# Two feed-forwards opened one token tile at a time, a gated unit's first step in two, modulation blocks at rate 1.0 in a downward product

## The reference, cut to what matters

```python
def first_block(...):                       # everything in float32
    for l in range(2):
        mod = silu(c) @ w_ada[l] + b_ada[l]             # 6 x 1024 numbers
        h = rms_norm(x, g_pre_mix[l]) * (1 + sc_m) + sh_m
        y = token_mixer(h, ...)                          # projections, two attentions, w_out
        x = x + gt_m * rms_norm(y, g_post_mix[l])
        h = rms_norm(x, g_pre_ffn[l]) * (1 + sc_f) + sh_f
        a = causal_depthwise_conv(h @ w_up_act[l], w_conv[l], b_conv[l])   # 3 taps over tokens
        y = (gelu(a) * (h @ w_up_lin[l])) @ w_down[l]    # 1024 -> 2816 -> 1024
        x = x + gt_f * rms_norm(y, g_post_ffn[l])

def _ffn_half(s, mod, g, wg, wu, wd):       # second network, 4 x 2 of these
    h = modulate(rmsnorm(s, g), shift, scale)
    return s + 0.5 * gate * ((silu(h @ wg) * (h @ wu)) @ wd)
```

## Time and profile before

| | |
|---|---|
| median of 3 runs | 2504.09 us (2496.96 to 2507.48) |
| the profiled execution | 2505.47 us, its span 2503.7 us |
| mean granted TensorE clock | 0.99 |
| TensorE matmul (PE) | 2418.9 us busy, 97%, 13166 instructions |
| weight loads (PEld) | 2036.0 us, 81% |
| VectorE (DVE) | 1676.1 us, 67% |
| ScalarE (ACT) | 1081.1 us, 43% |
| GpSimd (POOL) | 393.2 us, 16% |
| read from memory | 419.17 MB, 168 GB/s over the span |
| chain that ended last | PE 88%, DVE 6%, ACT 2%, issue 2%, POOL 1% |

### The profile page before, as it was taken

How to read it: one execution, slowest core, us unless ns; L and a number is a source line. 1 busy time by engine, 2 the same in 40 slices (tenths; PEclk the granted TensorE clock), 3 DMA queues, 4 the chain that set the end, 5 groups by cost and what they waited for, 6 DMA issues and landing times.

```text
span 2503.7 us, 34854 instructions
## 1 busy us (share of the span) xinstructions
PE 2418.9 (97%) x13166; PEld 2036.0 (81%) x13166; DVE 1676.1 (67%) x2618; ACT 1081.1 (43%) x1849; POOL 393.2 (16%) x431
## 2 busy tenths in 40 slices
PE   6999999989999999999979999999999999999998
PEld 5778987769989888887648888889888888777997
DVE  6967886869995776777955565565565556356554
ACT  4566545666554212237744322224322225345443
POOL 0211101111211201106850110100100110001101
PEclk9999999999999999999989999999999999999999
DMA  8656885556873554442112443442453443332662
GB/s 314 238 197 210 301 297 207 192 210 229 278 252 126 197 192 166 180 168 81 64 29 86 146 180 128 168 168 90 156 184 120 158 144 126 108 91 80 194 202 93
DMA packets 123336, 422.57 MB, mean 169 GB/s; under 512 B 15904, under 2 KB 20128, under 8 KB 123168
## 3 DMA queue, kind: packets, MB, share of 16 engines
q1 hardware_dynamic: 122608, 418.55, 48.2%
q10 hardware_dynamic: 560, 1.79, 0.2%
HBM read 419.17 MB, written 1.11 MB: 168 GB/s over the span
## 4 chain that ended last, share of the span: by engine, by line
PE 88%; DVE 6%; ACT 2%; issue 2%; POOL 1%; DMA 0%; DVEq 0%; ACTq 0%; POOLq 0%
PE ps L1159 27%; PE ps L1160 27%; PE ps L1161 27%; PE ps L1342 2%; PE ps L1354 2%; DVE sl L1705 1%; DVE mjunk L1719 1%; PE ps L1259 1%; PE ps L1322 1%; POOL ap L2226 1%; PE ps L1311 1%; ACT junk L1440 1%; DMA X<-in_x 0%; ACT F L1476 0%; DVE hL L1794 0%
## 5 line engine op out<-in xcount | busy, mean ns | idle before, releaser
L1417 ACT ACTIVATE sh<-raw 128x1024 fp32r<-128x1024 f32 x534 | 552.4, 1044 | 914.1 <-PE ps L1161 913.8
L1159 PE MATMUL ps<-hH,sh 128*128 128x256 f32 (+1 forms) x2560 | 840.8, 328 | 2.0 <-DVE hL L1794 2.0
L1161 PE MATMUL ps<-hH,sl 128*128 128x256 f32 (+1 forms) x2560 | 836.0, 327 | 0.0
L1160 PE MATMUL ps<-hL,sh 128*128 128x256 f32 (+1 forms) x2560 | 836.0, 327 | 0.0
L1705 DVE TENSOR_TENSOR sl<-raw,sh 128x1024 fp32r<-128x1024 f32 x534 | 640.3, 1219 | 107.0 <-ACT sh L1417 106.6
L1159 PEld LDWEIGHTS ps<-hH,sh 128*128 128x128 f32 x2560 | 481.4, 188 | 53.3 <-issue 5.6
L1160 PEld LDWEIGHTS ps<-hL,sh 128*128 128x128 f32 x2560 | 482.2, 188 | 49.3 <-issue 1.7
L1161 PEld LDWEIGHTS ps<-hH,sl 128*128 128x128 f32 x2560 | 481.2, 188 | 48.0
L1719 DVE CUSTOM_DVE_ANT_0 mjunk<-raw,cB,V 128x1024 bf16<-128x1024 f32 x384 | 499.2, 1300 | 26.6 <-DMA C<-in_cst 8.5
L2199 POOL TENSOR_TENSOR uLl<-F,uHh 128x256 fp32r<-128x256 f32 (+1 forms) x132 | 169.8, 1287 | 1172.1 <-ACT uHh L1594 1061.3
L1160 PE MATMUL ps<-sl,uHh 128*128 128x512 f32 x792 | 312.1, 394 | 0.0
(11 more groups left out here) (164 smaller groups left out, 2036.1 us busy)
## 6 DMA issues: line engine op xcount, KB each, us to landing
raw<-in_w SPq DMA_DIRECT2D x752, 512.0 KB, 4.6
G<-gates SPq DMA_DIRECT2D x14, 512.0 KB, 6.3
raw<-in_w SPq DMA_DIRECT2D x16, 256.0 KB, 4.4
cB<-in_rpb SPq DMA_DIRECT2D x64, 64.0 KB, 2.7
raw<-in_w SPq DMA_DIRECT2D x4, 492.0 KB, 6.7
S<-in_rows SPq DMA_DIRECT2D x6, 256.0 KB, 3.4
X<-in_x ACTq DMA_DIRECT2D x1, 1024.0 KB, 12.0
X<-in_ctx SPq DMA_DIRECT2D x1, 1024.0 KB, 5.9
```

The costliest lines, as they stand in the source:

```text
L1159: self.e.matmul(out, lh, rh, start=start, stop=False)
L1160: self.e.matmul(out, lh, rl, start=False, stop=False)
L1161: return self.e.matmul(out, ll, rh, start=False, stop=stop)
L1417: self.e.activation(self.m["sh"][k % SPL][:, 0:w], self.m["raw"][r % RAW][:, 0:w], ACT.Copy).then_inc(self.sems["w_hi"], 1)
```

## The change

Four parts.

- **Opening tile by tile** (`by_tile`). The first four chunks of both up products of the first layer's `ffn1`, and of gate and up of the last `ffn2`, are computed in the form of `down`: 8 units, tile 0 first, tile 1 behind it. Four banks of 128 tokens x 512 features per product come out; each is copied to SBUF (`utok`: tile 0 on ACT, tile 1 on DVE) and turned by four transposes (`uturn`) into the layout that the gated unit reads. `finish_norms` stands behind the third unit of tile 0. `warm(14)`, `warm(5)` become `warm(7)` in `ffn1` and `warm(14)` in `ffn2`.
- **Order before the first opening.** From the last use of a unit of `w_out` on (`hold`), no new unit is split until the plan says `ready`; tile 0's split (`second_parts`) moves ahead of tile 1's `gate2`; a `lower` is let out by `lowers`.
- **The gated unit of `ffn1`** (both layers): ACT's part (`glu1_a`) stands right behind the first product, DVE's part (`glu1_t`) is a step of its own behind the second. In layer 0 the gated units of chunks 0 to 3 are done beside the products of chunks 4 and 5, two beside each. In `ffn2` they stand ahead of the product of chunk 4.
- **Modulation blocks**: `RATES["down0"]` goes from 0.6 to 1.0. With four chunks fewer in the loop, `ffn1` of layer 0 has 18 calls of `pace(2)` where it had 22. `aside` starts with 6 empty items where it had 8, in both layers.

```diff
@@ RATES
-"down0": 0.6
+"down0": 1.0
@@ norm_tile(..., held=False)
         if early:
             self.second_parts()
+        if held:
+            self.add("lowers")
+            self.add("ready", n=1)
         ys = ...
         self.add("scale", ...)
@@ gate_half(..., held=False)
         self.first_parts()
         self.rms_close(st2[t], 2)
+        self.second_parts()
+        if held and t:
+            self.add("ready", n=1)
         for j in range(2):
             ...
-        self.norm_tile(hid, t, AB, 0, st, early=True)
+        self.norm_tile(hid, t, AB, 0, st, early=True, held=held and t)
@@ mixer, last product
                     part(kp, half, taken[(kp, half)], [i], i == 1, ...)
+                    if i and not half and kp == 2 and not l:
+                        self.add("hold", on=True)
-                self.gate_half(i, half, banks[half][i], gid, AB, hid, st2)
+                self.gate_half(i, half, banks[half][i], gid, AB, hid, st2, not l)
@@ new
+    def by_tile(self, names, hid, warm):
+        take = lambda n, j: self.unit(True, [n + (k, 0, 512) for k in (2 * j, 2 * j + 1)])
+        def part(n, j, t, b, last):
+            self.add("down", unit=n, ks=[2 * j, 2 * j + 1], tiles=[(t, (t, b))], last=last, full=b if j == 3 else None,
+                     act=("h", hid), nk=KD)
+        def stage(t, b, on):
+            S = self.place("S", 2 + t)
+            self.add("utok", b=b, S=S, on=on)
+            self.left(b)
+            return S
+        def turned(t, S, to):
+            self.add("uturn", S=S, t=t, to=to)
+        self.warm(warm)
+        self.add("hold", on=False)
+        one, two = ([take(n, j) for j in range(4)] for n in names)
+        A, B = [self.bank(), self.bank()], [self.bank(), self.bank()]
+        for j in range(3):
+            part(one[j], j, 0, A[0], False)
+        self.finish_norms()
+        part(one[3], 3, 0, A[0], False)
+        for j in range(2):
+            part(two[j], j, 0, B[0], False)
+        SA0 = stage(0, A[0], "a")
+        to = [self.bank(), self.bank()]
+        for j in range(4):
+            part(one[j], j, 1, A[1], True)
+            if j == 1:
+                turned(0, SA0, to)
+        for j in range(2):
+            part(two[j], j, 1, B[1], True)
+        SA1 = stage(1, A[1], "v")
+        for j in range(2, 4):
+            part(two[j], j, 0, B[0], False)
+        turned(1, SA1, to)
+        SB0 = stage(0, B[0], "a")
+        for j in range(2, 4):
+            part(two[j], j, 1, B[1], True)
+        up = [self.bank(), self.bank()]
+        turned(0, SB0, up)
+        SB1 = stage(1, B[1], "v")
+        return to, up, lambda: turned(1, SB1, up)
@@ ffn1
-        self.warm(14)
-        self.finish_norms()
-        self.warm(5)
-        self.aside += [lambda: None] * 8
+        done = 0
+        if l:
+            ...                                  # as before
+        else:
+            done = 4
+            to, up, rest = self.by_tile((("w_up_act", l), ("w_up_lin", l)), hid, 7)
+        self.aside += [lambda: None] * 6
-        for c in range(KF):
+        for c in range(done, KF):
             ba = self.product("w_up_act", l, c * 128, slice(0, 256), ("h", hid))
+            double = done <= c < done + done // 2
+            if double:
+                if c == done:
+                    rest()
+                while late:
+                    late.pop(0)()
+                begin(2 * (c - done), to[c - done], up[c - done], 0)       # glu1_a, glu1_t
+            else:
+                g = dict(...)
+                self.add("glu1_a", **g)
             if late:
                 late.pop(0)()
             bu = self.product("w_up_lin", l, c * 128, slice(0, 256), ("h", hid))
             if late:
                 late.pop(0)()
+            if double:
+                begin(2 * (c - done) + 1, to[c - done], up[c - done], 256)
+                late.pop(0)()
+                late.pop(0)()
+                begin(c, ba, bu, 0)
+            else:
+                g["bu"] = bu
+                finish(g)                                                   # glu1_t
-            self.add("glu1_a", **g)
             self.pace(2)
@@ ffn2, two tiles
-            self.warm(14)
-            self.finish_norms()
-            self.warm(5)
+            to, up, rest = self.by_tile((gate, up weights of this half), hid, 14)
@@ ffn2, loop over chunks
+                if len(tiles) == 2 and cc < 4:
+                    if c == 0:
+                        rest()
+                    ...                          # glu2_a of chunk c from to, up; glu2_b of chunk c-1
+                    continue
@@ finish
+            if s["kind"] == "hold":  held, more = s["on"], 0; continue
+            if s["kind"] == "ready": more += s["n"]
+            if s["kind"] == "lowers": out += lower; lower = []; continue
                     if split and len(order) >= SPL and order[-SPL] not in used:
                         break
+                    if split and held and not (real and n <= s["unit"]):
+                        if not more:
+                            break
+                        more -= 1
```

More of the change, by code:

```diff
@@ L225, in xs, with norm_tile @@
         return ("x", t, h, self.x_at[(t, h)])
-    def norm_tile(self, hid, t, AB, s, st=None, wide=False, lag=0, early=False):
+    def norm_tile(self, hid, t, AB, s, st=None, wide=False, lag=0, early=False, held=False):
         if st is None:
@@ L600, in ffn1 @@
                 late.pop(0)()
[L601 to L604 removed]
+            if double:
[5 more added lines that the diff above has]
+                g["bu"] = bu
+                finish(g)
             self.pace(2)
@@ L646, in ffn2 @@
                 begun = bool(head)
+                if len(tiles) == 2 and cc < 4:
+                    ba, bu, o = to[c // 2], up[c // 2], 256 * (c % 2)
+                    if c == 0:
+                        rest()
+                    g = dict(N=N, c=c, ba=ba, bu=bu, o=o, s=self.place("S", c % 2), f=self.next("F", 3), fid=fid, u=self.u_at)
+                    if late:
+                        late.pop(0)()
+                    self.add("glu2_a", **g)
+                    if c % 2:
+                        self.left(ba, bu)
+                    late.append(lambda g=g: self.add("glu2_b", **g))
+                    continue
                 if head:
@@ L653, in ffn2 @@
                         late.pop(0)()
-                g = dict(N=N, c=c, ba=ba, bu=bu, s=self.place("S", c % 2), f=self.next("F", 3), fid=fid, u=self.u_at)
+                g = dict(N=N, c=c, ba=ba, bu=bu, o=0, s=self.place("S", c % 2), f=self.next("F", 3), fid=fid, u=self.u_at)
                 if late:
@@ L919, in finish @@
         out, n, ctx, top, used, order, lower, loads = [], 0, False, 0, set(), [], [], []
+        held, more = False, 0
         for s in self.steps:
             real = "unit" in s and s["kind"] != "place"
+            if s["kind"] == "hold":
+                held, more = s["on"], 0
+                continue
+            if s["kind"] == "ready":
+                more += s["n"]
+            if s["kind"] == "lowers":
+                out += lower
+                lower = []
+                continue
             if real:
@@ L924, in finish @@
                 lower = []
-            if "unit" in s or "upto" in s:
+            if "unit" in s or "upto" in s or s["kind"] == "ready":
+                if s["kind"] == "ready":
+                    s["upto"] = len(self.units)
                 top = max(top, s["upto"] if "upto" in s else s["unit"] + 1)
@@ L1187, in warm, with uturn @@
         self.done("mm", ("left", s["b"]))
+    def uturn(self, s):
+        t, S = s["t"], self.buf(s["S"])
+        if t == 0:
+            for b in s["to"]:
+                self.wait_ge(self.gone(b))
+        self.wait_ge(self.got("tok", s["S"]))
+        for c in range(4):
+            o = 256 * (c % 2) + 128 * t
+            x = self.e.transpose(self.buf(s["to"][c // 2])[:, o:o + 128], S[:, c * 128:(c + 1) * 128],
+                                 self.m["C"][:, C_ID:C_ID + 128])
+        x.then_inc(self.sems["tr"], 1)
+        self.done("tr", ("left", s["S"]), *([("full", b) for b in s["to"]] if t else []))
     def proj(self, s):
@@ L1996, in oscale, with utok, glu1_t @@
         self.done("v_sb", ("os", s["mid"], s["kd"], s["i"]))
-    def glu1_a(self, s):
+    def utok(self, s):
+        if s["on"] != "v":
+            return
+        self.wait_ge(self.got("full", s["b"]))
+        self.wait_ge(self.gone(s["S"]))
+        self.e.tensor_copy(self.buf(s["S"])[:, :], self.buf(s["b"])[:, :]).then_inc(self.sems["v_ps"], 1)
+        self.done("v_ps", ("left", s["b"]), ("tok", s["S"]))
+    def glu1_t(self, s):
         l, c, fid = s["l"], s["c"], s["fid"]
-        S, pa = self.buf(s["s"]), self.buf(s["ba"])
+        S, pa = self.buf(s["s"]), self.buf(s["ba"])[:, s["o"]:s["o"] + 256]
         self.wait_ge(self.got("glu_a", fid, c))
```

47 lines of the change are left out of this document (34 added, 13 removed).

## The result

The changed kernel takes 2511.05 us (median of 8 runs, 2508.98 to 2514.55), the kernel before 2503.7 in the same session (8 runs, 2496.96 to 2507.48). The ratio is 1.003, its 95% interval 1.0018 to 1.0041: slower by 7 us. I had forecast 2497, with a range of 2488 to 2507.

A forecast was written before the change was run, and what follows sets the result against it. TensorE's matmuls, 88% of the chain of waits, were taken as the bound. First opening 5.6, second 1.7, `down` -0.5, layer 1's mixer 0.7 sum to 7.5: 2505.5 to 2498.0, less 1.4, say 2497; range 2488 to 2507.

The forecast's parts named there:

- Start of tile 0, wait for tile 1, W8: First opening: tile 0 starts at 199.15, tile 1 at 209.9 after waiting 1.3, chunk 4's first product (W8) at 225.4.
- Transposes: First opening: 24 transposes on TensorE at 0.11 us each, 2.64 in all; bounds 0.107 and 0.243 each.
- The rival of slow ones: Both openings: transposes take 0.243 each, losing 6.4, for 2503.0; chance 0.05.
- Made-up gated units: Beside chunks 4 and 5 of the first opening: three gated units each cost 1.0; bounds 0 and 7.0.
- the rival of splits run dry: Beside chunks 4 to 10, TensorE waits for splits and `down` begins without cover: 2507.0; chance 0.10.
- one of the signs that the prediction had named for being wrong: First opening: TensorE gaps named after `sl` between chunks 4 and 10, or tile 0's first matmul after 202.
- the 0.6 that the sum gave the form: First opening: eight units take 21.98 in the new 512-column form against 22.62 in the old, gaining 0.6.
- Last opening: Opening of the last `ffn2`: starts at 2310.95, W8 at 2335.6 in place of 2337.65; gain 1.7, bounds 0.3 and 2.1.
- `down` of layer 0 with 17 blocks: `down` of layer 0: 17 modulation blocks for 10 need 4% too much memory bandwidth; cost 0.5, bounds 0 and 2.2.
- Mixer of layer 1: Its last three blocks near 537.30 go, shortening TensorE's 1.94 wait for DVE's `hL`; gain 0.7, bounds -1.4 and 4.1.
- `glu1_a` in layer 1: Layer 1's `ffn1`: ACT's part ahead of gelu, with `aside` two items shorter, gains nothing; bounds -0.4 to 0.4.

The follow-up runs named there:

- e10: e9 with the first opening as before (both tiles together, nothing held, `down` of layer 0 at rate 0.6): 0.9994 of the kernel before.
- e9: e8 run again unchanged, for more runs and a second profile: 0.9941 of the kernel before.
- e5: Changed kernel with `down0` at 0.8048, so layer 1's mixer has its 20 old blocks at the old steps; far look-ahead kept: 0.9999 of the kernel before.
- e7: e5 with the engines' steps of the far look-ahead but weight loads in the order of the old one: 0.9996 of the kernel before.
- e2: Changed kernel with `ready` no longer raising the look-ahead for good, and `down0` at 0.8048 (20 blocks at old steps in layer 1's mixer): 0.9955 of the kernel before.
- e11: e9 with `down` of layer 0 at rate 1.0, so 17 blocks at other steps in layer 1's mixer: 0.9962 of the kernel before.
- e14: e8 with `down0` at 1.0 and layer 1's mixer keeping 17 blocks at the first 17 of the 20 old places: 0.9953 of the kernel before.
- e8: e2 with `hsplit` put ahead of `gate2` in layer 0 alone, no longer in layer 1: 0.9953 of the kernel before.
- e13: e8 with layer 1's gated unit whole again, both parts behind the second product's bank: 0.9946 of the kernel before.
- e12: e5 with layer 1's gated unit whole again, both parts behind the second product's bank: 1.005 of the kernel before.
- e4: The changed kernel run again unchanged, for a second profile: up of layer 1 took 124.6 us, layer 1's mixer 172.6.

## Why the prediction was wrong, step by step

- **Start of tile 0, wait for tile 1, W8.** Forecast 199.15, 209.9 after a wait of 1.3, and 225.4; measured 198.99, 210.02 after 0.92, and 225.10. Right.
- **Transposes.** Forecast 0.11 each; four take 0.35 from the first to the next matmul (224.75 to 225.10), 0.09 each. The rival of slow ones is out: the eight at 204.41 that gave its 0.243 ran at a granted clock of 0.50 (204.41 to 206.14), those at 194.55 at 1.00. The 275 ns of the Trainium skill ("TensorE: Matmul & The Clock Gate", Part 4: PE-mode transpose) do not speak against 0.11. The page gives them as the duration of one transpose, in bf16; the prediction added them up as if one began when the last had ended. The trace agrees with the page, in float32 (all sixteen of the first opening after; ns, shortest, median, longest):

```profile
L1311 PE MATMUL ps<-C,S x16: 270/272/273, 212.9 to 228.3; 128*128 128x128 f32 x16
```

- **Made-up gated units.** Forecast 1.0. With the old look-ahead TensorE has no wait at all from W8 to `down`. The opening's gain up to `down`, at one pitch, is 5.3 (e10 against e9), against 5.6. The changed kernel does wait there, 1.2 for two `sl`, as the rival of splits run dry would have it; but e5 and e7 have such waits and e2 and e9 none, so they come from the far look-ahead. The first of them, 0.62 at W16, is one of the signs that the prediction had named for being wrong. That 5.3 and 5.6 agree is in part luck: the 0.6 that the sum gave the form is a pitch (2.83 a unit is 0.1178 a matmul; at 0.1134 the eight old units take 21.77, less than the 21.98 of the new form), and the 1.0 for the made-up units did not come.
- **Last opening.** Forecast 1.7, measured 1.7.
- **`down` of layer 0 with 17 blocks.** Forecast 0.5; 67.86 against 67.87: nothing.
- **Mixer of layer 1.** Forecast a gain of 0.7, bound -1.4 if the blocks shift. This failed twice. The 17 blocks do not stay at the first 17 of the old places: in e11 eight of them stand at steps that had none, which costs 3.3 with the pitch out (against e9) and, under the far look-ahead, 0.0031 or 8 us by the ratios (after against e5). And even where they do stay (e14) nothing is gained, as the wait has a second releaser.
- **What was in no term.** The sum took `hold` and `ready` for edits of the first opening. `ready` raises the look-ahead for the rest of the program: 0.0044, 11 us (e5 against e2). And `second_parts` in `gate_half` has no condition, so that layer 1's opening got it too: 1.2 of wait (e2 against e9). Undoing both and the shift leaves a gain of 6.1 with the pitch out (e9), against 6.8, the sum's 7.5 without its 0.7 for the blocks. By the ratios it is 0.0047 to 0.0059 (e8, e9), 12 to 15 us: the rest is in no term, and whether it is pitch isn't shown.
- **`glu1_a` in layer 1.** Forecast nothing: right by itself (e13), but worth 0.005 beside the far look-ahead (e12 against e5).
- **The sums.** They were made against single profiles, and neither they nor the rivals knew the pitch, which makes up to 4.7 in one stage.

None of the rivals named the cause. The terms of the two openings came out within 1 us, one of them partly by luck; the miss is an edit whose reach was not followed, with the blocks that moved.

## What to carry to other kernels

When a planner is changed, write out every engine's order of before and after for the whole program and look at each stage where they differ, not only at those that the change names; a variable kept by `max` outlives the step that sets it. On an engine with little slack (DVE is busy 102.7 of 104 us in up 1), one more instruction ahead of what TensorE waits for can cost most of its own length (0.94 of 1.13 us here), the clock behind the wait, and perhaps the pitch of the rest of the stage. Compare traces of one stage only after its matmul pitch has been read in both.

## What the runs showed of the hardware

TensorE's steady matmuls have two pitches, at one granted clock (1.00) and in one order: 0.1134 or 0.1178 us at 256 columns, 0.2289 or 0.2334 at 512. Either way it is some 4.5 ns a matmul. Most stages keep what they started with. Of the changes seen within up 0 and up 1 all but one (e4, near 287) stand at a wait of TensorE, the shortest of 0.3 us (e5). In down 1 of after, e4, e5, e10 and e14 the pitch falls from 0.2334 to 0.2289 with no wait, at eight transposes in the middle of the stage (721.79 in after). Three stretches of e12's up 1, parted by waits of 1.18 (at 650.44) and 1.07 (at 668.10):

```profile
634.00:648.00 14.00, 13.54 (x115) 13.36 (x114) 11.98 (x19) 6.35 (x10) 1.48 (x2) 1.00 0.73 240
651.50:665.50 14.00, 14.00 (x126) 14.00 (x125) 11.97 (x19) 9.40 (x15) 2.63 (x3) 1.00 0.76 251
669.00:684.00 15.00, 15.00 (x130) 15.00 (x129) 12.94 (x21) 9.57 (x15) 2.61 (x3) 1.00 0.76 254
```

115 in 13.54 busy us are 0.118 each, 126 in 14.0 are 0.111, 130 in 15.0 are 0.115; the edges of a window cut into the count, and the distances from one matmul to the next are 0.118, 0.113 and 0.118. The sum over a whole run, 22 to 34 us above the lower pitch, differs by up to 12 between the traces here, which alone is of the size of the spread of one kernel's times. What draws it stays open. The Trainium skill ("TensorE: Matmul & The Clock Gate", Back-to-back issue gap) gives N / 2.4 + 2.5 ns for what it calls the isolated gap of a warm matmul, by estimate 109.2 at 256 columns and 215.8 at 512, and about 131 ns at 512 columns for a stream of weight loads and matmuls. Here, with weights loaded for each matmul, both pitches lie above all of these (228.9 and 233.4 at 512).
